# A small transformer stack in split float32r: weight rings of 12 and 8 blocks, and longer token-tile runs at the product boundaries

## The reference

```python
# layer 0: attention, adaLN modulation m = silu(c) @ w_mod[i] + b_mod[i] (six vectors of 1024)
hx = x * (1 + sc1) + sh1;  hc = ctx * (1 + csc1) + csh1          # 256 tokens each
q = rope(hx @ Wq); k = concat(hc @ Wk, rope(hx @ Wk)); v = concat(hc @ Wv, hx @ Wv)
a = softmax(q0 k0) - lam * softmax(q1 k1)                        # 8 heads, differential
x = layer_norm(ALPHA * x + g1 * (rms_heads(a @ v) @ w_o))
x = layer_norm(ALPHA * x + g2 * swiglu(x * (1 + sc2) + sh2))     # w_in 1024 x 5632, w_out 2816 x 1024
# layer 1: the same with a multi-scale pool (4 groups of 256) in place of attention
# block 3: rms_norm; u = x @ w_in_2 (1024 x 8208): gated linear attention and a block attention
# beside each other, each with a 1024 x 1024 output product and a gate, then w_out_2, + x
# x += relu(rms_norm(x) @ w_up_2) ** 2 @ w_down_2                (1024 x 4096, 4096 x 1024)
# x += sigmoid(rms_norm(x) @ w_ple_gate_2) * (p @ w_ple_2)
```

## Time and profile before

| | us |
|---|---|
| median of 3 executions (1250.66 to 1256.7) | 1253.57 |
| the profiled execution | 1245.34 |
| its span, first to last instruction | 1243.6 |

### The profile page before, as it was taken

How to read it: one execution, slowest core, us unless ns; L and a number is a source line. 1 busy time by engine, 2 the same in 40 slices (tenths; PEclk the granted TensorE clock), 3 DMA queues, 4 the chain that set the end, 5 groups by cost and what they waited for, 6 DMA issues and landing times.

```text
span 1243.6 us, 16451 instructions
## 1 busy us (share of the span) xinstructions
PE 1159.5 (93%) x6569; PEld 978.5 (79%) x6569; DVE 773.4 (62%) x867; ACT 574.1 (46%) x782; POOL 61.5 (5%) x118
## 2 busy tenths in 40 slices
PE   4999988989999996999999899999989989999987
PEld 2677855779988775899988687876878769998866
DVE  1566469587887779676554734546657665664454
ACT  2622338554434332444443546645764454553343
POOL 2011110001111101000000000000000000000000
PEclk8999989989999998999999989999999999999999
DMA  9965660449998864476556588876633345555540
GB/s 309 378 215 181 208 225 1 135 150 316 322 309 315 321 213 162 160 237 220 170 186 180 109 164 169 163 157 138 167 135 123 115 140 198 172 194 176 201 145 34
DMA packets 119429, 236.77 MB, mean 190 GB/s; under 512 B 5569, under 2 KB 60162, under 8 KB 119234
## 3 DMA queue, kind: packets, MB, share of 16 engines
q1 hardware_dynamic: 105458, 186.26, 49.7%
q0 software_dynamic: 13904, 49.56, 11.6%
HBM read 234.75 MB, written 1.05 MB: 190 GB/s over the span
## 4 chain that ended last, share of the span: by engine, by line
PE 82%; DVE 7%; ACT 4%; DMA 3%; issue 2%; SPq 2%; DVEq 0%; ACTq 0%
PE ps L1679 16%; PE ps L1680 16%; PE ps L1681 16%; PE ps L1716 8%; PE ps L1717 8%; PE ps L1718 8%; PE ps L1802 2%; DMA modraw<-in_w_mod 2%; PE ps L1944 1%; PE ps L1957 1%; DVE wL L1001 1%; ACT wH L557 1%; DMA mod<-in_w_mod 1%; DVE modraw L1080 1%; PE ps L1858 1%
## 5 line engine op out<-in xcount | busy, mean ns | idle before, releaser
L1001 DVE TENSOR_TENSOR wL<-raw,wH 128x1024 fp32r<-128x1024 f32 x328 | 399.9, 1223 | 340.0 <-ACT wH L557 338.6
L557 ACT ACTIVATE wH<-raw 128x1024 fp32r<-128x1024 f32 x328 | 345.8, 1058 | 460.1 <-PE ps L1681 321.8
L1679 PE MATMUL ps<-wH,aH 128*128 128x512 f32 (+1 forms) x576 | 233.5, 405 | 22.3 <-DVE aL L1029 8.8
L1716 PE MATMUL ps<-aH,wH 128*128 128x256 f32 x864 | 246.5, 285 | 1.6 <-DVE wL L1001 1.6
L1717 PE MATMUL ps<-aL,wH 128*128 128x256 f32 x864 | 244.5, 283 | 0.0
L1718 PE MATMUL ps<-aH,wL 128*128 128x256 f32 x864 | 244.5, 283 | 0.0
L1681 PE MATMUL ps<-wH,aL 128*128 128x512 f32 (+1 forms) x576 | 227.1, 394 | 0.0
L1680 PE MATMUL ps<-wL,aH 128*128 128x512 f32 (+1 forms) x576 | 227.1, 394 | 0.0
L1716 PEld LDWEIGHTS ps<-aH,wH 128*128 128x128 f32 x864 | 165.8, 192 | 2.8 <-DVE wL L1001 1.8
L1717 PEld LDWEIGHTS ps<-aL,wH 128*128 128x128 f32 x864 | 165.8, 192 | 1.1 <-issue 1.0
L1718 PEld LDWEIGHTS ps<-aH,wL 128*128 128x128 f32 x864 | 165.8, 192 | 0.0
(11 more groups left out here) (297 smaller groups left out, 1228.6 us busy)
## 6 DMA issues: line engine op xcount, KB each, us to landing
raw<-in_ffn_w_in SPq DMA_DIRECT2D x88, 512.0 KB
modraw<-in_w_mod POOLq DMA_DIRECT2D x80, 512.0 KB, 5.7
raw<-in_w_in SPq DMA_DIRECT2D x32, 1024.0 KB
raw<-in_ffn_w_out SPq DMA_DIRECT2D x22, 1024.0 KB
raw<-in_w_up SPq DMA_DIRECT2D x16, 1024.0 KB
raw<-in_w_down SPq DMA_DIRECT2D x16, 1024.0 KB
mod<-in_w_mod SPq DMA_DIRECT2D x8, 1024.0 KB, 12.1
raw<-in_attn_w_qkv SPq DMA_DIRECT2D x8, 1024.0 KB
```

The source lines that it names most:

```text
L557: nc.scalar.activation(wH[:, n % WS, :], raw[:, (n // 2) % RAW, (n % 2) * 1024:(n % 2) * 1024 + 1024], ACT.Copy).then_inc(w_hi, 1)
L1001: V.tensor_tensor(wL[:, n % WS, :], raw[:, (n // 2) % RAW, (n % 2) * 1024:(n % 2) * 1024 + 1024], wH[:, n % WS, :].bitcast(fp32), ALU.subt ...
L1679: T.matmul(outp, xh, h, start=first, stop=False)
L1716: T.matmul(dst, h, x_h[:, k, :], start=k == 0 and b % 2 == 0, stop=False, skip_group_check=True)
```

## The change

The low parts are written in place over the loaded weights: `wL` is laid at the address of `raw`, both now 12 blocks (6 slots), and `wH` has 8 blocks. SP's load of a pair therefore waits for `w_used` of the blocks that lay there, not for `w_lo`. ACT and DVE run 8 blocks ahead of PE in place of 4. `rows_mm` makes its last 8 blocks tile by tile (a product of 8 blocks wholly so), `first_mm` the first two chunks (8 blocks) of the next. The PE work that belongs to a boundary is hooked in at given places (`hooks`). `keep_warm` is gone. ACT and DVE put the 8 `adv` of a boundary between the steps of its normalisation. One modulation vector more (four) is made beside qkv, its last sum within the attention, and the others are moved; `ctxr` shares memory with `modraw`. The loops of SP, ACT, DVE and PE are written out. The memory for POOL's DMA descriptors goes from its default of 16384 bytes a partition to 4096.

```diff
-RAW, WS = 4, 4
+RAW, WL, WS = 6, 12, 8
...
-IN_QKV, IN_FF0, IN_FF1 = 3, 9, 10
-QKV_STEPS = {(c, j): (2, 2, 1, 1)[j] for c in range(2, 6) for j in range(4)}
-QKV_SELECT = {(3, 2): 0, (5, 0): 1}
-FF0_SELECT = {3: 3, 6: 4, 8: 5}
+IN_QKV, IN_FF0, IN_FF1 = 4, 9, 10
+QKV_STEPS = {(c, j): ((2, 2, 1, 1), (2, 2, 1, 1), (3, 3, 2, 2), (3, 3, 2, 2))[c - 2][j] for c in range(2, 6) for j in range(4)}
+QKV_SELECT = {(3, 3): 0, (4, 2): 1, (5, 1): 2}
+FF0_SELECT = {5: 4, 8: 5, 10: 6}
...
+        sLow = ExitStack()
+        wL = sb(sLow, "wL", [P, WL, 1024], f32r)
+        sLow.close()
         raw = sb(ctx, "raw", [P, RAW, 2048])
...
-                at_least(sp, w_lo, n - 2 * RAW + 2 + 8 * i if n >= 2 * RAW or not isinstance(i, int) else 0)
+                at_least(sp, w_used, n - WL + 2)
...
@@ ACT: ln; DVE's ln has its 8 adv at the like places @@
-                sd(k, 0)
-                adv(n)
-                adv(n + 1)
+                for j in range(sd_at):
+                    adv(n + j)
+                sd(k, 0)
+                for j in range(sd_at, 6 if k != 2 else 2):
+                    adv(n + j)
                 act.wait_ge(lncol_ready, min(norm, 1) + 1)
-                for j in range(2):
-                    hi_t(name, j, norm=norm)
+                hi_t(name, 0, norm=norm)
+                if k != 2:
+                    adv(n + 6)
+                hi_t(name, 1, norm=norm)
+                if k != 2:
+                    adv(n + 7)
...
@@ DVE: ln_pool @@
                 hat(0)
-                residual(1)
                 dve.wait_ge(ln_hat, TT + 1)
                 link(V.tensor_tensor(hm[:, 0, :], x[:, 0, :], sc1b[:, :], ALU.mult))
+                V.tensor_tensor(hm[:, 0, :], hm[:, 0, :], sh1b[:, :], ALU.add).then_inc(pool_h, 1)
+                adv(first + 1)
+                residual(1)
                 stats(1)
-                V.tensor_tensor(hm[:, 0, :], hm[:, 0, :], sh1b[:, :], ALU.add).then_inc(pool_h, 1)
...
-                adv(first + 1)
+                adv(first + 2)
+                hat(1)
                 low(0)
-                hat(1)
...
-                adv(first + 2)
-                adv(first + 3)
+                for j in range(3, 8):
+                    adv(first + j)
...
@@ DVE: beside out0 @@
+                    adv(SUBS[f"out{layer}"] + WS + k)
                     if layer == 0:
-                        if k in (2, 9, 17):
-                            vec_put({2: 6, 9: 7, 17: 8}[k])
-                        if k < 16:
-                            vec_steps(1)
+                        if k == 1:
+                            vec_put(6)
+                        elif k == 9:
+                            vec_put(7)
+                        vec_steps(1)
...
+                if layer == 0:
+                    vec_steps(2)
+                    vec_put(8)
...
@@ PE: rows_mm @@
-                single = 0 if tiled and kn <= KT else kn - 4 if tiled else kn
+                single = kn if not tiled else max(kn - WS, 0)
...
-                for k0 in range(single, kn, 4):
-                    for t in range(TT):
-                        for k in range(k0, min(k0 + 4, kn)):
+                for t in range(TT):
+                    for k in range(single, kn):
...
+                        ins = part(k, t)
+                        if t == 1:
+                            ins.then_inc(w_used, 1)
+                        elif k == kn - 1:
+                            ins.then_inc(tile0_done, 1)
...
@@ PE: first_mm @@
                 for t in range(TT):
-                    for s in range(4):
+                    for c in range(2):
+                        for s in range(4):
...
-                            elif s == 1:
+                            elif (c, s) == (1, 1):
                                 between()
...
-            rows_mm(SUBS["wo"], UNITS["wo"], aH, aL, KT, GROUPS["o"], between=o_last)
-            pe.wait_ge(ln_hat, 1)
-            tile_groups("x1", x, 0)
             pe.wait_ge(mod_out, NMOD0 + IN_QKV)
-            keep_warm(12)
+            rows_mm(SUBS["wo"], UNITS["wo"], aH, aL, KT, GROUPS["o"],
+                    hooks={(5, 0): o_last, (6, 1): tile_ready("x1", x, ln_hat, 1, 0)})
...
+                hooks = {(15, 0): lambda: vec_total(8)} if layer == 0 else {(20, 1): tile_ready("rms0", x, ln_hat, 3 * TT + 1, 0)}
...
-    nc = bacc.Bacc("TRN2", target_bir_lowering=False, num_devices=1)
+    nc = bacc.Bacc("TRN2", target_bir_lowering=False, num_devices=1, dynamic_dma_scratch_size=4096)
```

More of the change, by code:

```diff
@@ L633, in _ @@
                 hi(GROUPS["ctx"] + j, cH[:, 2 * j:2 * j + 2, :], mod=mc(j))
+            for j in range(12, 16):
+                adv(j)
             n = SUBS["qkv"]
@@ L771, in swiglu @@
                 one(2)
-                high(1)
-                with act.Fori(0, 4) as i:
-                    one(3, i)
-                    high(2, i)
-                    one(4, i)
-                    high(3, i)
+                hi(g + 1, hH[:, 2:4, :])
+                for c in range(3, 11):
+                    one(c)
+                    high(c - 1)
                 high(10)
-                for k in range(F1 // P - 2):
-                    adv(SUBS[f"out{layer}"] + 4 + k)
-            ln(0, SUBS["in0"] + 2, "x1")
+                for k in range(F1 // P - WS):
+                    adv(SUBS[f"out{layer}"] + WS + k)
+            ln(0, SUBS["in0"], "x1")
             swiglu(0)
-            ln(1, SUBS["in1"])
+            n = SUBS["pool"]
+            adv(n)
+            sd(1, 0)
+            for j in range(1, 8):
+                adv(n + j)
+            sd(1, 1)
             for j in range(4):
@@ L924, in _ @@
                 hi_t("ob", j)
-            for j in range(7):
-                adv(SUBS["brb"] + 4 + j)
-            hi_t("y", 0)
-            adv(SUBS["brb"] + 11)
-            for j in range(1, 4):
+            n = SUBS["wo2"]
+            for j in range(4):
+                adv(n + j)
+            for j in range(2):
                 hi_t("y", j)
-            for j in range(4):
-                adv(SUBS["wo2"] + 4 + j)
+            for j in range(4, 8):
+                adv(n + j)
+            for j in range(2, 4):
+                hi_t("y", j)
@@ L1246, in _ @@
                 lo_t("o", j, gain=subg)
-            for j in range(4):
-                adv(SUBS["wo"] + 4 + j)
             def lncol_of(k):
@@ L1426, in swiglu @@
                 one(2)
[L1427 to L1432 removed]
+                low_t(1)
+                for c in range(3, 11):
+                    one(c)
+                    low(c - 1)
                 low(10)
[L1434 to L1436 removed]
+                for k in range(F1 // P - WS):
+                    adv(SUBS[f"out{layer}"] + WS + k)
@@ L1456, in _ @@
             swiglu(1)
-            ln(3, "out1", g2b1, "rms0", [SUBS["win"] + j for j in range(4)])
+            ln(3, "out1", g2b1, "rms0", SUBS["win"])
             dve.wait_ge(t_done, GROUPS["rms0"] + 4)
@@ L1473, in rms @@
                     V.tensor_tensor(xt, pair(UNITS[stage] + t), xt, ALU.add).then_inc(acc_out, 1)
+                    if t == 1:
+                        lo_t(name, 1, gain=gain)
+                        for j in range(4, 7):
+                            adv(n + j)
                     dve.wait_ge(rms_sd, TT * k + t + 1)
@@ L1819, in tile_ready @@
                 return go
-            def keep_warm(count):
-                for _ in range(count):
-                    T.transpose(ps[:, 7, 0:P], ident, ident)
             def mod_mm(c):
@@ L1963, in _ @@
             scores(1)
-            vec_total(2)
             for r in range(16):
@@ L2149, in _ @@
             behind(0)
-            for c in range(1, 16):
-                chunk_mm(n + 4 * c, 0, [un + c], [X])
+            behind(1)
+            for c in range(2, 16):
+                chunk_mm(n + 4 * c, [un + c], [X])
                 behind(c)
```

535 lines of the change are left out of this document (245 added, 290 removed).

## The result

The changed kernel takes 1242.97 us (median of 8, 1239.75 to 1250.41) beside 1252.87 for the kernel before, ratio 0.9931 with a 95% interval of 0.9907 to 0.9956: 9.9 us faster. A second series on another occasion gave 1246.03 (median of 12) beside 1252.71, ratio 0.9961 (0.9937 to 0.9985): 6.7 us. It is faster, but the gain is a half to a third of the 20 us forecast.

A forecast was written before the change was run, and what follows sets the result against it. PE's stream of matmuls was taken as the bound, its waits and fill as what can be won. Gains of 29.3 us less losses of 9.5 gave net 19.8, from 1253.6 to 1233.8, stated as 1233, range 1214 to 1249.

The forecast's parts named there:

- sums 8 and 7 in out0: Waits at out0's modulation sums: 6.5 us and 1.0, against 2.2 before, less 1.7 for one sum fewer: 3.6 lost.
- Sums in qkv and attention: One more modulation sum in qkv, 1.7 us lost; the sum moved inside the attention, with DVE's extra step, 3.2 lost.
- Out1 to win: Boundary loss of 8.2 us falls to 1.8, less 1.0 for low-rank gate transposes; half of 3.4 clock saved: 7.1 gained.
- With 5.7 they land at T + 8.5: Next product's blocks 4 and 5, requested at T + 2.8 (T: tile 0 whole), take 5.7 us; 1.8 wait left.
- Rival 1: Weight loads come late at the boundaries: at 10.6 us a load, 15 us less gain, 1248; chance 0.11.
- wo to in0: Boundary loss of 7.9 us falls to 1.8 and the 1.6 wait at wo's start goes: 7.7 gained.
- wo2 and up: Boundary from brb and wo2 to up: loss of 5.0 us falls to 0.5, 0.5 elsewhere in brb: 5.0 gained.
- down to pg and ple: Boundary loss of 3.9 us before pg falls to 0.5, 3.4 gained; gate ready for ple, 0.9 gained.
- bra to brb: DVE's chain at this boundary stays as it is; 1.0 us lost to the clock (0 to 3.4).
- rival 2: Clock falls at six boundaries where fill is gone: 17.7 us less gain, 1251, no change; chance 0.08.
- Rival 3: Smaller descriptor memory stops POOL's vector loads overlapping: 125 us slower, 1360, or 13 in qkv with two; chance 0.09.
- the 51.3 us of the boundaries: PE time counted as lost in five boundary stretches before the change: 7.9, 26.3, 8.2, 5.0 and 3.9 us.

The follow-up runs named there:

- sum78: Changed kernel with sum 8 moved to block 21, sum 7 between block 9's token tiles, three DVE row operations to blocks 10 to 12: 1229.33 us, ratio 0.9818.
- sum8: Changed kernel with only sum 8 of out0 moved from ahead of block 14 to ahead of block 21 of tile 0: 1236.11 us, ratio 0.9861.
- att: sum8 with sum 3's last two steps moved, one into qkv, one behind attention's first two maxima: 1233.1 us, ratio 0.9846.
- six1: sum8 with the last six blocks by token tile in out1 alone, instead of eight: 1232.09 us, ratio 0.9843.
- nofill: Kernel before the change with its 93 fill transposes left out, nothing else: 1252.13 us, ratio 0.9995.
- fillpool: sum8 with fill transposes at the pool stage (20, 85 and 20): 1232.24 us, ratio 0.9845.

## Why the prediction was wrong

- **The step that failed: sums 8 and 7 in out0**, "that is 6.5, plus 1.0 at sum 7 ...: 3.6 lost". The chain was right: the load behind step 69, the last step, PE standing one half-block in. Each number was too small: the load took 6.85 and 7.47 us where 5.7 was taken, so the wait was 8.1 and 8.8 in place of 6.5; sum 7 waited 2.9 in place of 1.0, since the three row operations that put DVE 3.7 us behind were not counted (0.8 to 1.0 is what is left without them, see sum78); and the clock, which falls at both, was put at nothing there and took 7 us. Out0 lost 15.0 us where this term had 3.6; with in0's rest, which gained 3.1 for the 1.2 counted, it is 11.9 and not 2.4. sum8 and sum78 take back 9.9 us in the medians and 5.4 by the ratios.
- **Sums in qkv and attention**: 8.0 lost where the forecast had 3.3. In the attention the term of 3.2 was right: PE stands 6.6 us for the first exponentials where it stood 5.2 with the sum in between, and the sum comes later at 1.8. The 2.2 more of the stage's 3.8 is no more than its clock varies (80.74 and 84.06 us in two profiles with before's code). att shows that the two steps ahead of DVE's maxima are 2.6 of the 6.6. In qkv PE idles 1.4 us more than before (at its sums 1.1 and 0.4), and the rest of the 4.2 is work; this was not tried.
- **Out1 to win, the other step that failed**: 0.9 gained where the forecast had 7.1. "With 5.7 they land at T + 8.5" took a median of POOL's loads of 512 KB for a 1 MB pair, of which two are under way. Rival 1 holds here (12.4 and 12.9 us against its 10.6); six1 takes back 3.1 us. At in0 it did not hold: the wait there is under 2 us. The other half is clock: 47 instructions of the low-rank gate (x824 to x871 in win's rest, 5.6 us at 0.12) only moved from win's first eight blocks to its rest, and the rest took 8.9 us more, 3.3 beyond these instructions, with 6.8 us at half clock where before has none (3.4 to 10.2 in the other profiles).
- **Right in kind**: wo to in0 (8.2 for 6.1 at in0), wo2 and up, down to pg and ple (12.4 and 12.7 in the two profiles for 9.3), pool to in1 (3.3 for 4.0), DVE's time in place, POOL's loads. Before the first matmul of in0 PE waits 1.6 us at most, of up and pg under 1.4. Why three boundaries gave 5.5 us more than counted was not traced; in0's first eight have no half clock now and had 6.8 us of it. At bra to brb the 1.0 lies between the 0 of the two profiles and the 2.5 us that half of the profiles of these kernels show there.
- **Rivals 2 and 3**: nofill speaks against rival 2, the clock where fill was taken, though on the kernel before; in the changed kernel it is left at the pool, where fillpool takes back 2.8 us. Rival 3 is out: 6.1 us a load, and no step in qkv waits as it would have it.
- **The sign of the clock was wrong**: it was to fall only round the pool and after the low-rank products, and it fell in qkv, the attention and out0 too.
- **The sum**: it leaves out two terms of its own, forms (1.2 gained) and transposes (1.9 lost), 0.7 together; and the 51.3 us of the boundaries, called "without the clock", hold the half clock inside the five stretches.

The boundaries gave some 25 us, as much as was worked out for them, but by luck: win's 6.2 too few and the 5.5 too many of three others cancel. The stages between them, out0 above all, took back 14 more than was counted.

## What to carry to other kernels

When the run-ahead of a ring is bounded by what PE has used, everything that stands between its copies in an engine's order is late with it: place a sum by the time its last operand can be there, and look at the last of its loads first, sized by its own bytes and with those asked for beside it. Longer runs by token tile cover a norm, but they free the slots all at once; the length at which the two costs meet (at out1 six did best among four, six and eight) is to be tried per boundary. Of fill, only that which reached to 1.5 us of the end of a long wait shortened its stage here; that which left 2.6 us did not, and 93 transposes spread over the boundaries of the kernel before gained nothing.

## What the runs showed of the hardware

- Loads of `w_in` run at 171 to 180 GB/s with the DMA engines full (0.88 to 1.01), whereas out0's stretch has 306 to 313 GB/s at 0.84 to 0.88. The rows don't tell why. The Trainium skill ("DMA: Bandwidth & Descriptors", "Specifications") gives about 358 GB/s as the limit of HBM per core; an estimate by that is 5.9 us for two pairs, and 12.4 and 12.9 were measured.
- The granted clock fell at the waits of 2.90, 4.03, 8.13 and 10.8 us, with 6 us of fill ahead of one of them or not; behind bra, where PE waits 2.2 us, it fell in seven of the twelve profiles of kernels without fill there and not in the other five, with the same instructions. Executions of one kernel differ by 3 to 14 us (before's 24 runs: 1244.37 to 1258.08).
